# Hybrid SSD/HGRN2/attention step: transposes and step-size sums of the SSD opening moved into the projection

## What is computed

```
proj = h @ w_in                                  # z, xbc, dt and the HGRN2 columns
xbc = silu(dwconv(xbc, conv_w, conv_b))          # width 3 along the tokens
xs, bm, cm = split(xbc)                          # x: 16 heads of 64; B, C: 2 groups of 128
dt = softplus(dt_raw + dt_bias); a = -exp(a_log)
A = dt * a; A_cs = cumsum(A) within each chunk of 128 tokens
decay_states = exp(A_cs[-1] - A_cs)
states = einsum(B, decay_states, x * dt)         # one chunk state per chunk and direction
new_states = running sum of states, each decayed by exp(chunk total of A)
y = (C B^T * L) x dt  +  C new_states exp(A_cs)  +  d_skip * xs
y_ssd = rms_norm(y * silu(z))
```

## Time and profile before

| | |
|---|---|
| median of three runs | 2337.45 us |
| the profiled execution | 2336.06 us, of which its span is 2334.3 us |
| TensorE busy | 2197.8 us, 94% of the span |
| VectorE, ScalarE, GpSimd busy | 1379.9, 906.1, 174.2 us |
| mean granted TensorE clock over the span | 0.976 |

### The profile page before, as it was taken

How to read it: one execution, slowest core, us unless ns; L and a number is a source line. 1 busy time by engine, 2 the same in 40 slices (tenths; PEclk the granted TensorE clock), 3 DMA queues, 4 the chain that set the end, 5 groups by cost and what they waited for, 6 DMA issues and landing times.

```text
span 2334.3 us, 33569 instructions
## 1 busy us (share of the span) xinstructions
PE 2197.8 (94%) x13797; PEld 1915.0 (82%) x13797; DVE 1379.9 (59%) x1967; ACT 906.1 (39%) x1803; POOL 174.2 (7%) x213
## 2 busy tenths in 40 slices
PE   6889899999998889999999999998999999999998
PEld 4768868878877878799999988886556798999997
DVE  4457483356227486676556546786775774655655
ACT  4445373245225463442222223544554632222222
POOL 0000000034005201100000000200000200000002
PEclk8989999999999999999999999997999999999999
DMA  7401205511640111322222222211000131322221
GB/s 311 174 32 51 86 6 199 192 48 55 225 181 10 67 61 72 109 84 71 82 75 71 82 73 64 80 55 41 1 1 1 46 99 58 97 71 74 73 72 45
DMA packets 43702, 192.23 MB, mean 82 GB/s; under 512 B 4992, under 2 KB 4992, under 8 KB 36640
## 3 DMA queue, kind: packets, MB, share of 16 engines
q1 hardware_dynamic: 41328, 176.86, 21.8%
q0 software_dynamic: 2224, 13.24, 1.6%
HBM read 182.47 MB, written 7.60 MB: 81 GB/s over the span
## 4 chain that ended last, share of the span: by engine, by line
PE 61%; DVE 5%; ACT 2%; issue 1%; DMA 0%; POOL 0%; ACTq 0%; DVEq 0%; POOLq 0%
PE pg L1022 31%; PE pg L1061 18%; PE ps L1257 2%; PE pg L1237 2%; PE pg L721 2%; PE ps L870 2%; PE pg L1212 1%; PE ps L1212 1%; PE ps L768 1%; DVE mxs L2377 1%; PE pg L870 1%; DVE rtb L1838 1%; PE ps L1081 0%; DVE xlo L1812 0%; PE ps L1179 0%
## 5 line engine op out<-in xcount | busy, mean ns | idle before, releaser
L1022 PE MATMUL pg<-hh,xhi 128*128 128x320 f32 (+2 forms) x1008 | 313.5, 311 | 9.8 <-DVE hl L1926 9.8
L1022 PE MATMUL pg<-hl,xhi 128*128 128x320 f32 (+2 forms) x1008 | 311.4, 309 | 0.0
L1022 PE MATMUL pg<-hh,xlo 128*128 128x320 f32 (+2 forms) x1008 | 311.4, 309 | 0.0
L1812 DVE TENSOR_TENSOR wlo<-ring,whi 128x1024 fp32r<-128x1024 f32 x127 | 154.7, 1222 | 194.7 <-ACT whi L1300 194.4
L721 PE MATMUL pg<-hh,whi 128*128 128x320 f32 x848 | 207.2, 326 | 13.7 <-DVE wlo L1812 13.2
L1300 ACT CAST whi<-ring 128x1024 fp32r<-128x1024 f32 x127 | 132.1, 1047 | 206.4 <-PE pg L1061 136.4
L1022 PEld LDWEIGHTS pg<-hh,xhi 128*128 128x128 f32 x1008 | 191.5, 190 | 12.5 <-issue 12.3
L1022 PE MATMUL pg<-hh,whi 128*128 128x320 f32 (+1 forms) x640 | 197.6, 309 | 0.0
L1022 PE MATMUL pg<-hh,wlo 128*128 128x320 f32 (+1 forms) x640 | 196.7, 307 | 0.0
L1022 PE MATMUL pg<-hl,whi 128*128 128x320 f32 (+1 forms) x640 | 196.6, 307 | 0.0
L721 PE MATMUL pg<-hl,whi 128*128 128x320 f32 x848 | 195.0, 312 | 0.0
(11 more groups left out here) (347 smaller groups left out, 4702.4 us busy)
## 6 DMA issues: line engine op xcount, KB each, us to landing
ring<-in_wstream SPq DMA_DIRECT2D x229, 512.0 KB, 3.6
adaring<-in_wada SPq DMA_DIRECT2D x21, 1024.0 KB, 4.9
ybuf<-in_wada SPq DMA_DIRECT2D x21, 1024.0 KB, 4.9
adabig<-in_wada SPq DMA_DIRECT2D x6, 1024.0 KB, 17.1
xk<-in_x SPq DMA_DIRECT2D x2, 1280.0 KB, 9.6
yssd_scratch<-ybuf POOLq DMA_DIRECT2D x2, 1280.0 KB, 5.8
xk<-yssd_scratch POOLq DMA_DIRECT2D x1, 2560.0 KB, 10.2
xk<-in_x_tok POOLq DMA_DIRECT2D x1, 2560.0 KB, 10.4
```

What stands on the lines that cost most here:

```text
L1022: last = nc.tensor.matmul(out, w[:, k * P:(k + 1) * P], h[:, k, a:b], start=k == 0 and m == 0, stop=k == KT - 1 and m == 2)
L1812: V.tensor_tensor(lo, flat(ring[:, s % RING]), hi.bitcast(F32), ALU.subtract).then_inc(wlo_ready, 1)
```

## The change

- A new function `ssd_turn(g, i)` on TensorE, called after each of the tiles i = 0 to 6 of a group's projection (six convolution tiles and z0). By the table `SSD_TURNS` it transposes B after tile i = 2, and x's feature tiles 0 to 3 after i = 3, 4, 5 and 6. Each turn is five blocks of 128 tokens of one feature tile, through the two banks `ps[:, 0:2]` together. It waits for the convolution concerned (c + 1 of the group) and, past the first, for the evacuation of the turn before (`xt_done`).
- The step-size sums (`step_sums`) stand right behind the turn of B. In group 1 they wait for the last use of their bank by group 0 (`cb_used`).
- On ScalarE `ssd_turned(g, i)` evacuates each turn in one copy of 128x640 (for x, strided into `xtok`), right behind the Silu of tile i and in front of the cast of the slot after next; the exponent for the decays follows B's copy. The four scaled copies into `ybuf` come after all of this. For x3 the copy stands behind the evacuation of z0.
- The 24 steps of z1 to z3 are dealt out by `SSD_FILL`: four in front of the first chunk state and behind the wait for `mod_ready`, then 2, 3, 2, 3, 2, 3, 2, 3 behind the eight.
- VectorE's order is untouched; the condition for its first `xw` is `xt_done` in place of `tr_done`. The two transposing jobs of the attention part are numbered 0 and 1 in place of 14 and 15.

```diff
+SSD_TURNS = {2: 0, 3: 2, 4: 3, 5: 4, 6: 5}
+SSD_FILL = (4, 2, 3, 2, 3, 2, 3, 2, 3)
...
-            def ssd(g, z1):
-
-                pe.wait_ge(conv_done, 6 * (g + 1))
+            def ssd_turn(g, i):
+
+                if i not in SSD_TURNS:
+                    return
+                n, c = 5 * g + list(SSD_TURNS).index(i), SSD_TURNS[i]
+                pe.wait_ge(conv_done, 6 * g + c + 1)
+                if n:
+                    pe.wait_ge(xt_done, n)
+                src = bcT[:, 0] if c == 0 else xsT[:, c - 2]
+                bank = ps[:, 0:2].rearrange("p a b -> p (a b)")
+                for tt in range(TT):
+                    last = nc.tensor.transpose(bank[:, tt * P:(tt + 1) * P], src[:, tt * P:(tt + 1) * P],
+                                               cm[:, IDENT, :])
+                last.then_inc(xt_ready, 1)
+                if c == 0:
+                    step_sums(g)
+
+            def step_sums(g):
+
                 pe.wait_ge(dt_ready, 1)
-                j = 7 * g
-                tok = lambda t: slice(t * P, (t + 1) * P)
-                transposes(j, [bcT[:, 0, tok(t)] for t in range(4)])
-                transposes(j + 1, [bcT[:, 0, tok(4)]])
-                for t in range(TT):
-                    transposes(j + 2 + t, [xsT[:, i, tok(t)] for i in range(4)])
+                if g:
+                    pe.wait_ge(cb_used, len(SSD_UNITS) // 2)
...
+            def ssd(g, z1):
+
+                def fill(n):
+
+                    a = sum(SSD_FILL[:n])
+                    b = a + SSD_FILL[n]
+                    while a < b:
+                        c = min(b, (a // KT + 1) * KT)
+                        gemm(z1 + a // KT, steps=(a % KT, a % KT + c - a))
+                        a = c
+
                 pe.wait_ge(mod_ready, 2)
+                fill(0)
                 for n, (d, t) in enumerate(SSD_STATES):
...
                     nc.tensor.matmul(ps[:, 3, :], btok[:, t, :], xw, start=True, stop=True).then_inc(ls_ready, 1)
-                    a, b = ((n % len(SSD_STATES)) * 3, (n % len(SSD_STATES) + 1) * 3)
...
+                    fill(n % len(SSD_STATES) + 1)
...
-                for _ in range(6 if g == 0 else 7):
+                for i in range(1 if g == 0 else 0, 7):
                     gemm(t)
+                    ssd_turn(g, i)
...
-            def tr_evac(j, dst, n):
-                act.wait_ge(tr_ready, j + 1)
-                nc.scalar.copy(dst, ps[:, j % 2, 0:n]).then_inc(tr_done, 1)
+            def ssd_turned(g, i):
+
+                if i not in SSD_TURNS:
+                    return
+                n, c = 5 * g + list(SSD_TURNS).index(i), SSD_TURNS[i]
+                act.wait_ge(xt_ready, n + 1)
+                bank = ps[:, 0:2].rearrange("p a b -> p (a b)")[:, 0:NT].rearrange("p (t n) -> p t n", t=TT)
+                dst = btok[:] if c == 0 else xtok[:, :, (c - 2) * P:(c - 1) * P]
+                nc.scalar.copy(dst, bank).then_inc(xt_done, 1)
+                if c == 0:
+                    act.wait_ge(dsum_ready, g + 1)
+                    nc.scalar.activation(dect[:].rearrange("p a t h -> p (a t h)"), ps[:, 2, 0:4 * TT * HPG],
+                                         ACT.Exp).then_inc(dexp_ready, 1)
...
                     nc.scalar.activation(dst[:, SAMPLE:NT], b, ACT.Silu).then_inc(conv_done, 1)
+                    ssd_turned(g, i)
...
                 evac(t, zs[:, 0], ACT.Silu)
+                ssd_turned(g, 6)
                 prep(t + 1)
...
-                dve.wait_ge(tr_done, 7 * (g + 1))
+                dve.wait_ge(xt_done, 5 * (g + 1))
```

More of the change, by code:

```diff
@@ L473, in hybrid_step @@
         tr_done = sem("tr_done")
+        xt_ready = sem("xt_ready")
+        xt_done = sem("xt_done")
         s0_in = sem("s0_in")
@@ L807, in ssd @@
                 last.then_inc(dsum_ready, 1)
+            def ssd(g, z1):
+                tok = lambda t: slice(t * P, (t + 1) * P)
+                def fill(n):
[5 more added lines that the diff above has]
+                        a = c
                 pe.wait_ge(mod_ready, 2)
+                fill(0)
                 for n, (d, t) in enumerate(SSD_STATES):
@@ L814, in ssd @@
                     if d == 0 and t == PROMPT_TT:
-                        pe.wait_ge(tr_done, 7 * (g + 1))
+                        pe.wait_ge(xt_done, 5 * (g + 1))
                     nc.tensor.matmul(ps[:, 3, :], btok[:, t, :], xw, start=True, stop=True).then_inc(ls_ready, 1)
-                    a, b = ((n % len(SSD_STATES)) * 3, (n % len(SSD_STATES) + 1) * 3)
[L818 to L821, removed]
+                    fill(n % len(SSD_STATES) + 1)
                 pe.wait_ge(st_ready, (g + 1) * len(SSD_STATES))
@@ L1196, in _ @@
             pe.wait_ge(kv_in, 16 * 5)
-            transposes(14, [ck[:, kv].rearrange("p a b -> p (a b)") for kv in range(KV_HEADS)])
-            transposes(15, [ak[:, kv, SAMPLE:NT] for kv in range(KV_HEADS)])
-            pe.wait_ge(tr_done, 16)
+            transposes(0, [ck[:, kv].rearrange("p a b -> p (a b)") for kv in range(KV_HEADS)])
+            transposes(1, [ak[:, kv, SAMPLE:NT] for kv in range(KV_HEADS)])
+            pe.wait_ge(tr_done, 2)
             for b in range(2):
@@ L1388, in ssd @@
                 last.then_inc(yd_ready, 1)
[L1389 to L1395, removed]
                 for i in range(1, 4):
@@ L1755, in _ @@
             tr_evac_k = (ak[:, :, NT:NT + P], kout[:])
-            act.wait_ge(tr_ready, 15)
+            act.wait_ge(tr_ready, 1)
             nc.scalar.copy(tr_evac_k[0], ps[:, 0, :].rearrange("p (k t) -> p k t", k=KV_HEADS)).then_inc(tr_done, 1)
-            act.wait_ge(tr_ready, 16)
+            act.wait_ge(tr_ready, 2)
             nc.scalar.copy(tr_evac_k[1], ps[:, 1, :].rearrange("p (k t) -> p k t", k=KV_HEADS)[:, :, 0:HD]).then_inc(tr_done, 1)
@@ L2371, in _ @@
                     rope_apply(i - 2)
-            dve.wait_ge(tr_done, 16)
+            dve.wait_ge(tr_done, 2)
             def att_max(p):
@@ L2521, in _ @@
             G.dma_start(cs[:, 1], rope[:, 1]).then_inc(kv_in, 16)
-            pool.wait_ge(tr_done, 16)
+            pool.wait_ge(tr_done, 2)
             G.dma_start(k_out, kout[:]).then_inc(kv_out, 16)
```

## The result

| | before | changed |
|---|---|---|
| median | 2337.21 us (2336.39 to 2337.83, four runs) | 2324.08 us (2321.32 to 2327.72, four runs) |
| ratio | | 0.9945, interval 0.9932 to 0.9958 |
| the profiled execution, its span | 2336.06, 2334.3 us | 2327.72, 2325.9 us |

The kernel is faster by 13.1 us. The profiled execution is the slowest of its four, so the trace has only 8.4 us of gain in its span to account for.

The account below looks back on a forecast made before the run. TensorE, busy nearly the whole span, was taken as the bound, its opening holes costing kernel time. Gains of 3.5 and 8.7 us, together 12.2, off the profiled 2336.06 gave 2323.9, hence a median of 2325.2; range 2319 to 2331.

Parts of the forecast that it names:

- Turns and sums push z0 back: Among the convolution tiles: four transpose turns and the step-size sums delay z0's end by 3.11 us a group.
- Copies, load and exponent ahead of the cast: ScalarE's queue: cost nothing, 0.34 us spare at the third tile; rival dear table switch, 2326.1 us, chance 0.02.
- Group 0's hole: After group 0's z0, TensorE stands still 3.26 us for VectorE's bias add, four steps queued behind.
- The clock behind it: Group 0's hole brings one fall to 1.2 GHz, costing 1.62 us; rival no fall, 2323.6 us, chance 0.12.
- 9.35, bound 9.4: Group 0's first state starts 9.35 us after z0 ends; bounds 5.4, if the add is no obstacle, and 9.4.
- Group 0's saved state: Group 0, first to third state: 7.2 us, with a 1.1 us wait because the second saved copy awaits the first's DMA.
- 6.5 and 6.6 as the bound: Group 1, first to third state: 6.5 us taken, bounds 6.12 and 6.6, its saved-state DMA needing at most 4.14.
- Group 1's first state: Group 1: first state 4.90 us after z0 ends, with a 0.85 us wait left because VectorE does the rest first.
- The other states: Third state's start to z3's end: 19.70 us, plus 0.3 or 0.4 for starts; fourth and seventh states cost 3.73.
- The sum: Openings, z0's end to z3's: 36.6 and 31.5 us, 12.2 us gained over both groups.
- Behind the openings: Stages after z3 keep their length; rival given back, a later wait takes all the gain, 2337 us, chance 0.04.

Follow-up runs that it names:

- experiment 1: The changed kernel with TensorE's wait for `mod_ready` moved behind the four steps in front of the first state; 2319.18 us, ratio 0.9925.
- experiment 3: The changed kernel with the last fillers of `SSD_FILL` 3, 3, 2 in place of 3, 2, 3; 2322.76 us, ratio 0.9941.
- experiment 7: The changed kernel with a buffer of its own (half of `xd`) for the second saved state; 2321.78 us, ratio 0.9935.
- experiment 2: The changed kernel with VectorE's weight rest for z2's slot moved behind the gate step and the first `xw`; 2321.65 us, ratio 0.9935.
- 12: The changed kernel repeated unaltered, to profile the HGRN2 part again; one execution, 2328.46 us.
- experiment 6: The kernel before with the new `SSD_FILL` steps alone, transposes and sums left behind z0; 2328.49 us, ratio 0.9962.

## Why the prediction was right

The forecast was 2325.2, between 2319 and 2331; measured 2324.08. The sign, the place and the size hold, but three terms were off, not all to one side, and one loss was not forecast; that the median lies within 1.1 us of the forecast is in part luck.

- *Turns and sums push z0 back.* Forecast 3.11. Group 0's z0 ends 114.46 - 59.77 = 54.69 us behind the turns of the step-size tile, in place of 111.48 - 59.71 = 51.77: 2.92 later. Between group 0's z3 and group 1's z0 lie 109.49 us in place of 106.84, 2.65 more, or 3.18 once the 0.53 is put back by which the part between z3 and the written result became shorter (60.72 against 61.25). Right.
- *Copies, load and exponent ahead of the cast.* Nothing was forecast, with 0.34 us to spare at the third tile. ScalarE began with that tile at 229.68, and the rest ended at 238.32, 8.64 us later against 8.75 forecast; TensorE needed it at 238.46, 8.78 later against 9.09. So 0.14 us were left of the 0.34, and TensorE's waits for rests ahead of these steps stayed at 13.2 us. The drain that the Trainium skill adds ("ScalarE: Activation LUTs", section "What ACT_TABLE_LOAD costs") did not show: load 1.28 us, exponent 0.01 behind it.
- *Group 0's hole.* Forecast 3.26, measured 3.09, ended by VectorE's bias add, and shown by experiment 1. Right.
- *The clock behind it.* Here the price was too low: "a fall costs 1.62". In six profiles with this hole, the four steps took 6.33, 6.27, 6.41 and 5.16 (the changed kernel), 3.63 (experiment 3) and 5.16 (experiment 7). Against 3.52 the fall cost up to 2.9 us, or nothing. The first state came at 10.57 where 9.35, bound 9.4, was forecast. The step that failed was to take one fall, seen once in one place, as the price and the upper bound of any: there the slow stretch behind the first state was over after at most 3.4 us (1.00 again from 127.70), here it lasts 6.0 us from the end of the hole to 124.70.
- *Group 0's saved state.* "7.2, a wait of 1.1" did not come: first to third state took 6.13, TensorE's own time. "But VectorE's second saved state waits for the DMA" was right, but I took the 4.77 us of the earlier trace rows as what that DMA always takes, and here it was 3.64. The slow landing was in the other group: copy to copy 4.92, first to third state 7.43 where I took 6.5 and 6.6 as the bound. Experiment 7 shows that this wait is the DMA. Why it was the slow one is argued only: the DMA engines were 82% busy over it and 19% over group 0's, and no run moved the other transfers. Together the two terms nearly cancel (13.56 against 13.7), which is luck.
- *Group 1's first state.* Forecast 4.90 with a wait of 0.85; measured 4.76 and 0.53.
- *The other states.* From the third state to the end of z3 19.70 and up to 0.4 for the starts was forecast; measured 20.10 and 20.19. The waits before the eighth state are 0.94 and 0.96.
- *The sum.* Openings 36.6 and 31.5 were forecast, 36.80 and 32.38 came. At the end of group 1's z3 the profile stands 11.7 us ahead of before, against 12.2.
- *Behind the openings* I expected nothing to change. The HGRN2 part's first group is 2.9 to 3.6 us longer in all four profiles of the changed kernel (the two groups together 1.1 to 3.1), and those executions took 2327.72, 2326.08, 2326.29 and 2328.46 us, all above the forecast. The median of 2324.08 lies so near to it because the other three runs took 2321.32 to 2325.65. Their mean granted clocks were 0.981, 0.979 and 0.978, the highest in the fastest, against 0.977 in the profiled one; where those runs were spared a fall, no trace shows.

## What to carry over

Ask of every wait in a hand-written order what it guards, and put it right in front of that: fill work that is moved ahead of a wait for data must be moved ahead of the other waits there too, or it inherits them (5.3 us in group 0, for one line). When fill closes one gap, look at what is late next: here the single save buffer and its DMA, which had been hidden, and then a weight rest in front of short work. A price read from one slow stretch is one sample, not a bound. Clock falls can lie elsewhere afterwards in stages that the change does not touch, so compare milestones over the whole program, and repeat the profile before a difference of 3 us far behind the change is put down to it or to chance.

## What the runs showed of the hardware

- The same hole of 3.09 us, in the same place, was followed by a fall to the 1.2 GHz level at once (6.27 to 6.41 us for four steps), a little later (5.16) or not at all (3.63); against the 3.52 of full clock that is between 0.1 and 2.9 us. The Trainium skill ("TensorE: Matmul & The Clock Gate", section "What's actually happening") says that the activity monitor runs free and is not started by the kernel, which agrees with the varying place. It does not tell why the hole of 2.29 us in the HGRN2 part took the same side in every profile of a kernel, and no run here does.
- Shorter waits were followed by falls too: one of 1.88 us in experiment 2, and one of 2.09 us ahead of all that was changed, at 70 us, in two of the 14 profiles (experiments 3 and 12, granted clock 0.50 from 71 to 74 us), where z0 of group 0 then ended 56.2 us behind the turns of the step-size tile in place of 54.7. Those of 1.05 and 0.96 us in group 1 of the first trace were not.
- The DMA of a saved state (256 KB) let its waiter go 3.59 to 5.77 us after the copy into the buffer began, group 0 of experiment 6 and group 1 of experiment 2 being the ends; the DMA share was 0.19 over the 3.64 us and 0.82 over the 4.92 us of the changed kernel.
- The end of group 0's z0 lay between 109.32 and 111.48 us in three profiles of the kernel before: some 2 us of scatter arise ahead of everything that was changed.
